# All projections but the index queries in token form, with their turning on GpSimd, SyncE and ScalarE

## The reference

```
h = rms_norm(x, norm_gain)
qa, ka, va, ga, qb, kb, vb, gb, qi, ki, wi = split(h @ w_in)
out_a = chunked_relpos_attention(qa, ka, va, rel_bias)     # own and 8 earlier chunks of 64
out_b = dsa_sparse_attention(qb, kb, vb, qi, ki, wi)       # indexer, top 64 keys of a query
y = concat(out_a * silu(ga), out_b * silu(gb))
x = x + y @ w_out
return rms_norm(x, final_gain)
```

## Time and profile before

| | us |
|---|---|
| median of three runs | 521.57 |
| the profiled execution | 520.91 |
| its span, first to last instruction | 518.8 |
| PE busy | 509.6 |
| DVE busy | 364.7 |
| ACT busy | 306.1 |
| POOL busy | 31.1 |

### The profile page before, as it was taken

One profiled execution on the slowest core, in us unless ns is written; L12 is line 12 of the kernel. 1 busy time (PEld: TensorE's weight loads), 2 busy tenths in 40 slices (PEclk: granted clock), 3 DMA queues, 4 the chain that ended last, 5 costly groups with the idle time before them and its releaser, 6 DMA issues.

```text
span 518.8 us, 7543 instructions
## 1 busy us (share of the span) xinstructions
PE 509.6 (98%) x2736; PEld 442.2 (85%) x2736; DVE 364.7 (70%) x544; ACT 306.1 (59%) x415; POOL 31.1 (6%) x47
## 2 busy tenths in 40 slices
PE   8999999999999999999999999999999999999994
PEld 6989999888888888888888888888888878888883
DVE  5798776775856787867776776687878778646554
ACT  6876555446564554445675849495868676544342
POOL 1000054140400000000000000000000000000000
PEclk9999999999999999999999999999999999999999
DMA  8984787758795776553956575665647875576614
GB/s 276 356 261 134 241 262 257 245 176 244 230 271 163 251 215 222 179 190 99 284 145 228 158 228 167 190 192 163 198 159 231 288 230 171 195 207 200 198 42 162
DMA packets 83933, 107.79 MB, mean 208 GB/s; under 512 B 26400, under 2 KB 68288, under 8 KB 83648
## 3 DMA queue, kind: packets, MB, share of 16 engines
q1 hardware_dynamic: 82320, 101.92, 63.3%
q0 software_dynamic: 1296, 5.01, 3.0%
q10 hardware_dynamic: 288, 0.46, 0.2%
HBM read 99.24 MB, written 2.11 MB: 195 GB/s over the span
## 4 chain that ended last, share of the span: by engine, by line
PE 97%; DMA 1%; DVE 0%; issue 0%; ACT 0%; DVEq 0%; POOLq 0%
PE acc L506 28%; PE acc L475 14%; PE acc L477 14%; PE acc L476 14%; PE acc L510 14%; PE acc L526 4%; PE acc L534 3%; PE aux L536 2%; PE aux L658 1%; PE aux L667 1%; DMA gain<-norm_gain 1%; PE aux L655 0%; PE aux L656 0%; PE aux L673 0%; PE aux L654 0%; PE aux L672 0%
## 5 line engine op out<-in xcount | busy, mean ns | idle before, releaser
L1068 DVE TENSOR_TENSOR lo_slots<-raw_slots,hi_slots 128x1024 fp32r<-128x1024 f32 x166 | 204.7, 1240 | 105.1 <-ACT hi_slots L735 103.8
L735 ACT ACTIVATE hi_slots<-raw_slots 128x1024 fp32r<-128x1024 f32 x166 | 174.3, 1056 | 140.7 <-PE acc L477 91.3
L506 PE MATMUL acc<-acts,hi_slots 128*128 128x512 f32 (+1 forms) x640 | 195.5, 387 | 0.0
L510 PEld LDWEIGHTS acc<-acts,lo_slots 128*128 128x128 f32 x640 | 119.3, 188 | 22.7
L475 PE MATMUL acc<-hi_slots,acts 128*128 128x512 f32 x320 | 124.9, 390 | 0.7 <-issue 0.7
L476 PE MATMUL acc<-lo_slots,acts 128*128 128x512 f32 x320 | 124.6, 389 | 0.0
L477 PE MATMUL acc<-hi_slots,acts 128*128 128x512 f32 x320 | 124.5, 389 | 0.0
L510 PE MATMUL acc<-acts,lo_slots 128*128 128x256 f32 (+1 forms) x640 | 123.8, 275 | 0.0
L506 PEld LDWEIGHTS acc<-acts,hi_slots 128*128 128x128 f32 x640 | 97.4, 189 | 0.1
L475 PEld LDWEIGHTS acc<-hi_slots,acts 128*128 128x128 f32 x320 | 60.1, 188 | 13.0 <-issue 0.9
L477 PEld LDWEIGHTS acc<-hi_slots,acts 128*128 128x128 f32 x320 | 60.1, 188 | 12.6
(11 more groups left out here) (179 smaller groups left out, 478.0 us busy)
## 6 DMA issues: line engine op xcount, KB each, us to landing
raw_slots<-w_blocks SPq DMA_DIRECT2D x140, 512.0 KB, 4.4
raw_slots<-wo_blocks SPq DMA_DIRECT2D x32, 512.0 KB, 4.2
raw_slots<-w_blocks SPq DMA_DIRECT2D x8, 256.0 KB, 5.3
qk<-x POOLq DMA_DIRECT2D x1, 2048.0 KB, 10.7
qk<-xT SPq DMA_DIRECT2D x7, 256.0 KB, 5.3
o<-ext_dram POOLq DMA_DIRECT2D x1, 1024.0 KB, 10.0
fgain<-final_gain POOLq DMA_DIRECT2D x1, 1024.0 KB, 8.0
out<-o SPq DMA_DIRECT2D x2, 512.0 KB, 3.0
```

The costliest lines, as they stand in the source:

```text
L506: nc.tensor.matmul(whole, w_hi4[:, u % RING, q, f * HD:f * HD + HD], acts[:, k, :, tokens], start=(k == 0), stop=False)
L510: last = nc.tensor.matmul(acc[:, bank:bank + n], w_lo4[:, u % RING, q, f * HD:f * HD + HD], a_hi[:, k, tokens], start=False, stop=(k == KT ...
L735: nc.scalar.activation(hi_slots[:, s, 0:UK * CB], w_raw[:, s, :], ACT.Copy).then_inc(hi_done, 1)
L1068: nc.vector.tensor_tensor(lo_slots[:, s, 0:UK * CB], w_raw[:, s, :], hi_slots[:, s, 0:UK * CB].bitcast(f32), ALU.subtract).then_inc(lo_don ...
```

## The change

Blocks 10 to 17 go over to token form, and their eight results are turned as those of blocks 4 to 7 are. What the feature form needed there is gone: the two copies, adds and rate products a block, and the making of `rk`. The late results are numbered n = 4 to 11.

- The separation into planes of n = 4 to 11 stands on POOL, eight copies of 128 x 2048 uint16. For n = 8 to 11 (gates) source and target are `v1` and `t_gate`, for 4 to 7 the second half of `o`.
- `projection_out(g)` stands on ACT after the split of the next block's unit 2. The join of the block before stands in `turned_back(pair - 1)`, behind the exponentials and two splits of the next pair, followed there by `output(pair - 1)` and for gates by one tanh of 128 x 1024.
- SP issues the transposing DMA of a late result after the load of unit 6 of the next block, and the one of the probabilities after the load of unit 2 instead of ahead of it.
- The residual `x` is loaded by POOL in two DMAs: the first 512 columns of both token tiles once all pairs are scored, the rest after the last transposing DMA.
- Blocks 17 and 18 have a new order of splits, gates, `y_hi` and `y_lo`. The loops over pairs are written out.

```
+            def split_projection(n):
+                pool.wait_ge(proj_out, n + 1)
+                nc.gpsimd.tensor_copy(proj_planes(n)[0], halves(z)).then_inc(proj_split, 1)
+                pool.wait_ge(proj_split, n + 1)
+
+            for n in range(N_LATE, N_END):
+                split_projection(n)
+                if n == N_END - 2:
+                    pool.wait_ge(scored, HEADS)
+                    pool.dma_start(x_rows[:, :, 0:CB], x[:, :, 0:CB]).then_inc(res_landed, 16)
+            pool.wait_ge(proj_turned, 16 * N_END)
+            pool.dma_start(x_rows[:, :, CB:D], x[:, :, CB:D]).then_inc(rest_landed, 16)
...
             for pair in range(HEADS):
                 g = pair + G_QKA
-                pe.wait_ge(feat_out, 2 * g - 17)
-                feature_unit(g, 0)
-                if pair > 0:
-                    value_pair(pair - 1)
-                feature_unit(g, 1)
...
+                if pair < 2:
+                    both_out(pair + 3)
+                else:
+                    pe.wait_ge(proj_out, pair + N_LATE - 1)
+                for u in range(UNITS):
+                    unit(g, u)
+                    if u == 0 and pair > 0:
+                        value_pair(pair - 1)
+                    if u == 1:
+                        pe.wait_ge(proj_joined, (4, 4, 4, 4, 7, 7, 8, 8)[pair])
+                        score_pair(pair, 2 * pair + 1 if pair < 4 else pair)
...
+            def turned_back(pair):
+                join_projection(pair + N_LATE)
+                act.wait_ge(proj_joined, pair + N_LATE + 1)
+                output(pair)
+
+            def pair_attention(g, pair, staged):
+                exps(pair, pair < 4)
                 split_hi(g, 6)
+                planes_out(pair)
                 split_hi(g, 7)
+                if pair > 0:
+                    turned_back(pair - 1)
+                if pair > 4:
+                    tanh_gates(pair - 5)
                 split_hi(g, 8)
                 split_hi(g, 9)
+                stage_q(*staged)
+                pT_out(pair)
                 split_hi(g, 10)
+                if pair > 4:
+                    act.wait_ge(y_done, 2 * (pair - 4))
+                projection_out(g)
```

More of the change, by code:

```diff
@@ L290, in halves, with proj_planes, proj_home, feature_use @@
             return flat(words[:, :, :]).bitcast(u16).rearrange("p (n s) -> p s n", s=2)
[L292 to L301, removed]
+        PROJ_WORDS = 4 * T
+        def proj_planes(n):
+            if n < N_GATE:
+                at = D * (n >= N_LATE)
+                pair = (o_flat[:, at:at + PROJ_WORDS], o_flat[:, at + PROJ_WORDS:at + 2 * PROJ_WORDS])
+            else:
+                pair = (v1_flat[:, 0:PROJ_WORDS], flat(t_gate[:, :, :]))
+            return [t.bitcast(u16).rearrange("p (s n) -> p s n", s=2) for t in pair]
+        def proj_home(n):
+            if n >= N_GATE:
+                return halves(z).rearrange("p s (c n) -> p s c n", c=2)
+            first, step = ((0, 2), (4, 2), (1, 2), (5, 2), (0, 1), (2, 1), (4, 1), (6, 1))[n]
+            return qk[:, :, :].bitcast(u16).rearrange("p c (n s) -> p s c n", s=2)[:, :, first:first + step + 1:step, :]
+        def feature_use(g, half):
+            return 2 * (g - G_QI) + half
         def narrow_loads(p):
@@ L369, in turn_planes, with feature_block, token_block @@
                                        flat(planes)).then_inc(planes_turned, 16)
-            def feature_block(g, row, turned=None):
+            def feature_block(g, row):
                 for u in range(UNITS):
-                    if u == 2 and turned is not None:
-                        turn_planes(turned)
                     sp.wait_ge(lo_done, g * UNITS + (u - RING + 1))
                     load_features(u, w_blocks[ds(row, 1), :, :, :].rearrange("o u p c -> p (o u) c"))
-            def token_block(g, row, turned=None):
+            def token_block(g, row, pair=None, n=None):
                 for u in range(UNITS):
@@ L976, in gate_block, with tanh_gates @@
[L976 to L998 removed]
+            def tanh_gates(i):
+                act.wait_ge(proj_joined, i + N_GATE + 1)
+                nc.scalar.activation(flat(t_gate[:, :, :]), flat(z[:, :, :]), ACT.Tanh, scale=0.5).then_inc(tanh_done, 1)
@@ L1496, in y_lo @@
+                pT_rest(pair)
+                for c in range(10, 14):
+                    split_lo(g, c)
             def y_lo(q):
@@ L1500, in y_lo @@
                                         a_hi[:, UK * q:UK * q + UK, :].bitcast(f32), ALU.subtract).then_inc(ylo_done, 1)
-            gate_block(G_OUT - 1, 3, False)
-            for q in range(4):
-                y_lo(q)
+            g = G_OUT - 1
+            probabilities(HEADS - 1)
+            split_lo(g, 6)
+            split_lo(g, 7)
+            gated(2, 0)
+            gated(2, 1)
+            split_lo(g, 8)
+            y_lo(0)
+            y_lo(1)
+            split_lo(g, 9)
+            y_lo(2)
+            y_lo(3)
+            split_lo(g, 10)
             pT_rest(HEADS - 1)
-            gate_out(G_OUT - 1, 3, 1)
             split_lo(G_OUT, 3)
```

245 lines of the change are left out of this document (84 added, 161 removed).

## The result

The change makes the kernel faster by half a per cent: a median of 518.84 us (518.41 to 520.19, 6 runs) against 521.75 us (521.09 to 522.43, 6 runs) of the kernel before on the same chip, ratio 0.9947 (95% interval 0.9932 to 0.9961). The forecast was 527.3 us, slower. The profiled execution took 518.86 us, span 517.0, against 520.91 and 518.8. The later kernels were timed beside the kernel before too, which took 521.3 to 521.4 there instead of 521.75; so medians of different rounds can lie 0.4 us apart without any cause in the kernel.

A forecast was written before the change was run, and what follows sets the result against it. The prediction took PE's instructions, busy 98% of the span, to bound the kernel. Its terms -4.2 + 6.0 + 3.9 = +5.7 on 520.91 gave 526.6, with the median 0.66 above: 527.3 us, range 517.5 to 537.

The forecast's parts named there:

- What goes: Blocks 10 to 17 in token form save PE 0.065 us x 8 units x 8 blocks, 4.2 us.
- X: Duration of POOL's copy of 128 x 2048 uint16, taken as 2.7 us, with 1.8 and 4.8 as ends.
- the selection: Earlier POOL instruction, one input and one output, 128 columns in 0.29 us; its rate gave 2.7 us for 2048.
- The ring: Attention chain from one pair's turned probabilities to the next's: 22.7 + X = 25.4 us against PE's 24.1; waits sum to 6.0.
- That the copy holds the splits: In the ring, POOL's copy and DVE's three two-input splits exclude each other, so X counts in full.
- The seam: Block 18: PE waits 1.6, 1.3 and 1.7 us at units 0, 2 and 6, less 0.7 there before: 3.9 us.
- The 1.3 at unit 2: Block 18: last gates' copy starts between two DVE instructions and holds unit 2's split, so PE waits 1.3 us.
- The first: Rival: the copy doesn't hold the ring, being near the lower end or with splits slipping in; 518.2 us, chance 0.33.
- The prediction's line for X = 1.8 with full exclusion: Under the first rival: ring waits of 0.6 us and a seam of 2.2, giving 520.1 us.
- Two tensors' rate: Rival: POOL's copy takes 4.8 us, ring 27.5, +22.6 us, 544 us in all; chance 0.08.
- Token form is cheaper: Answers the rival that token form is no cheaper here: gain of 4.2 missing, 531.5 us; chance 0.04 with late turning.
- The turning: Rival: transposing DMA lands over 11.6 us after the copy, each us over costing 6; chance 0.04 with the token-form rival.

The follow-up runs named there:

- the forecast's copy: Changed kernel with a second POOL copy of 860 words of 4 bytes ahead of each of the eight, the two running 2.74 us: 523.96 us, ratio 1.0053.
- each alone: Changed kernel with the last of the eight copies on DVE: 519.28 us; changed kernel with the last transposing DMA ahead of unit 6's load: 518.88 us.
- both together: Changed kernel with the last transposing DMA ahead of unit 6's load and the last copy on DVE: 517.84 us, ratio 0.993.

## Why the prediction was wrong

*What goes: 4.2 us on PE.* Right in kind, 3.8 measured, eight times 0.47.

*X, the copy: taken as 2.7, measured 1.90.* This is the step that failed, and it decided the sign. The bounds of 1.8 and 4.8 held it, but the choice within them went by the selection of the earlier trace rows, a row of 128 columns. The rate wasn't what was wrong: a copy of 128 columns takes 0.30 us, the selection 0.29. But from 128 to 2048 columns the copy grows by 1.60, 0.83 ns each, which leaves 0.19 for the fixed part, and the prediction took 0.13, from a fill of one column. Over so short a row that small error makes the 0.8 us: with 0.19, if the selection has it too, the same row gives 1.8. The lower end, iota, was right to 0.1 us by luck: it used the same 0.13. By the prediction's own "one us of X is worth 8 us" this error is 6.4 us. With the forecast's copy the kernel does lose: 523.96 against 518.84, 5.1 us for 0.84, so 6.1 us per us (6.6 by the ratios to the kernel before), as pairs 1 and 4 had room for a part.
The Trainium skill (GPSIMD Engine Reference, section Elementwise — side-by-side cycle accounting) has about 1.8 cycles an element as the best case of a tight loop, an estimate of 3.1 us at 1.2 GHz; the measured 1.90 stands against it for this copy. The same section has 1.03 cycles for loop bodies of few operations, an estimate of 1.76 us; with that the trace agrees, at 0.83 ns an element and a fixed part.

*The ring: 22.7 + X forecast, 22.3 + X measured*, at two lengths of X, of which 2.74 is the test, since at 1.90 PE's block gives the same sum. Three splits behind the copy take 3.27, not 3.5, as the recorded duration of a group runs past the next one's start; exponential to the end of `pT_out` 14.44, not 14.6; the rest rounding. The pattern over the pairs was forecast as 0.35, 1.3, 1.3, 0.3, 1.35, 1.35 and came at the forecast's copy as 0.31, 0.65, 0.89, 0.10, 0.90, 0.95: the same shape, 0.4 less at pairs 3, 5 and 6, which is the 0.4 of the ring. Pair 2 is 0.65 less; ahead of it DVE got a split in between the two copies (the second lasted 2.96 us there and 1.89 later). Of the 3.3 us between the forecast's 527.3 and the 523.96, these waits are 2.2. At the real copy both errors together take the ring from 25.4 to 24.2, and PE's block stands at 24.15.

*That the copy holds the splits* was right, and both directions of the earlier trace rows came again: the splits took 4.39 us instead of 3.50 behind the copy, and the last copy 3.57 instead of 1.90 behind DVE. A fill that reads nothing does not hold them.

*The seam.* At the forecast's copy units 0 and 6 idle 1.60 and 1.68 us, where 1.6 and 1.7 stood; at the real one 0.21 and 0.82. The match at unit 6 is in part luck: its DMA landed after 4.3 us instead of 4.9, and PE came there 0.8 us earlier than forecast. The 1.3 at unit 2 never came, with either copy, and is most of the rest of those 3.3 us: I let POOL enter between two DVE instructions. It doesn't here. Its copy became ready at 422.35, and DVE ran what it had back to back:
```profile
421.74 1.29 DVE L1458 TENSOR_TENSOR acts<-o,acts 128x512 fp32r<-128x512 f32 x2
422.95 1.22 DVE L1075 TENSOR_TENSOR lo_slots<-raw_slots,hi_slots 128x1024 fp32r<-128x1024 f32 x1
424.83 1.63 DVE L1419 TENSOR_TENSOR parts_lo<-probs_T,parts_hi 128x512 fp32r<-128x512 f32 x1 [0.67 <-ACT parts_hi L954]
```
```profile
422.35 3.57 POOL L481 COPY v<-z 128x2048 uint16<-128x2048 uint16 x1 [17.41 <-ACT z L868]
```
POOL waits until the split ends at 424.17 and then needs its 1.8 us; what it holds is `pT_rest` (1.63 instead of 0.69), which nobody is waiting for yet.

*The rivals.* The first, given 0.33, is what happened in its number (518.2 against 518.84) and half in its reason: its copy was to be "up to 1.9 us or no exclusion"; it is 1.9 us, with exclusion. The prediction's line for X = 1.8 with full exclusion, 520.1, has the mechanism that was seen. It is 1.3 us too high: the seam was 2.2 us net there, against 0.2 + 1.0 - 0.7 = 0.5 measured, and the gain on PE, 3.8 instead of 4.2, works the other way. Two tensors' rate did not come. Token form is cheaper. The turning made ACT wait only at the last turn, 2.09 us, for a DMA that took 4.81, as forecast; what the prediction didn't have among its steps is that a load right ahead of it would have taken back an earlier issue.

What stays open: why the transposing DMA behind a load lands at nearly one time whenever it is issued (6.72, 5.48 and 4.81 us after issue), when POOL gets in between two DVE instructions and DVE between two of POOL's, and how much of each median's last 0.5 us is the start of the program, which differs by 1.1 us between the profiled executions.

## What to carry to other kernels

Where a new instruction enters a ring that is within a microsecond of the bottleneck's step, forecast the ring at both ends of the unknown duration and give the chance to the step between them; here 0.8 us of one copy, eight times repeated, turned 2.9 us gained into 2.7 lost. For an engine's rate take two lengths of one instruction; a short row and a fixed part borrowed from another instruction missed by 0.8 us of 1.9 here. Where an earlier producer brings nothing, read the chain of waits again at that place: at the seam two causes covered each other, and each alone was worth nothing that the time shows (519.28 and 518.88), both together 1.0 us. And where taking a cost away changes no time, look whether a wait behind it has grown: without the copy, the one at unit 6 grew by what the others gave.

## What the hardware showed

- A POOL copy of 128 x 2048 uint16 out of a stride of two takes 1.90 us, one of 128 such half-words 0.30, of 2048 words of 4 bytes 1.91, of 860 such words 0.91; a fill of 2048 half-words takes 1.81. So in these rows the count of elements sets the time, and neither their size nor the read does (0.1 us). DVE needs 1.22 for the same copy.
- A POOL copy that was under way held DVE's splits, which have two inputs, until it ended (three in 4.39 us instead of 3.50); a fill, which only writes, did not. Between DVE instructions that follow each other without a gap POOL was not let in, over 1.8 us; even the copy of 128 half-words took 1.96 us at that place instead of 0.30. Between two POOL copies that follow each other DVE was let in in some blocks (second copy 2.89 and 2.96 us) and in others not (1.89).
- The last transposing DMA took 1.32 us to issue and 4.5 to land with no load right ahead of it, and 4.72 and 6.72 with one of 512 KB issued 0.4 us before.
- The best kernel that came of this is the changed one with the last transposing DMA ahead of the load and the last copy on DVE, 517.84 us, ratio 0.993 to the kernel before (0.9916 to 0.9943); with all copies on DVE it is the same.
